# One decoder layer step: the sample tile's output products ahead of attention, from unsplit w_out rows, and the first full tile's products in attention's last turns

## The reference

```
proj = rmsnorm(x) @ w_in                      # q, k, v (8 heads x 64), b, c, u (512 channels each)
attn = dilated sliding-window attention       # windows (128,1) (512,4) (2048,16), merged by their sums
conv = b * conv3(c * u)
o    = concat(rmsnorm(attn, g_a), rmsnorm(conv, g_c)) @ w_out
x    = x + o
x    = x + moe(rmsnorm(x))                    # top-1 of 4 groups, top-2 of its 8 experts of width 512
y    = rmsnorm(x)
```

## Time and profile before

| | us |
|---|---|
| median of 3 runs | 1086.1 (1084.65 to 1086.41) |
| the profiled execution | 1085.33 |
| its span, first to last instruction | 1083.1 |
| PE busy in the span | 1051.1 (97%) |
| DVE busy | 448.0 (41%) |
| ACT busy | 272.8 (25%) |
| mean granted clock of PE | 0.994 of full speed |

### The profile page before, as it was taken

How to read it: one execution, slowest core, us unless ns; L and a number is a source line. 1 busy time by engine, 2 the same in 40 slices (tenths; PEclk the granted TensorE clock), 3 DMA queues, 4 the chain that set the end, 5 groups by cost and what they waited for, 6 DMA issues and landing times.

```text
span 1083.1 us, 19546 instructions
## 1 busy us (share of the span) xinstructions
PE 1051.1 (97%) x8052; PEld 684.3 (63%) x8052; DVE 448.0 (41%) x1100; ACT 272.8 (25%) x594; POOL 130.3 (12%) x167
## 2 busy tenths in 40 slices
PE   7999999999999999999999999999999999997987
PEld 6899999999967767888744433444434444443323
DVE  5414546233167657888864421212211111111156
ACT  7212221110137863323121111111111111111114
POOL 1001211002100000000112111121111112021010
PEclk9999999999999999999999999999999999999999
DMA  8216776234144206113999999999999999999987
GB/s 256 79 39 159 167 189 162 70 119 137 60 137 156 83 28 275 40 78 126 397 369 410 407 419 420 420 418 422 419 418 420 418 419 418 419 418 419 422 341 310
DMA packets 111133, 294.73 MB, mean 272 GB/s; under 512 B 43874, under 2 KB 68602, under 8 KB 86146
## 3 DMA queue, kind: packets, MB, share of 16 engines
q1 hardware_dynamic: 61634, 245.00, 56.9%
q0 software_dynamic: 14960, 40.03, 10.7%
q10 hardware_dynamic: 34448, 8.42, 3.5%
HBM read 276.38 MB, written 32.07 MB: 285 GB/s over the span
## 4 chain that ended last, share of the span: by engine, by line
PE 81%; DMA 7%; SPq 7%; DVE 3%; issue 1%; ACT 1%; DVEq 0%; POOLq 0%; ACTq 0%
PE psum L1292 15%; PE psum L916 9%; PE psum L918 8%; PE psum L917 8%; PE psum L1350 7%; SPq L782 6%; PE psum L1306 5%; PE psum L1050 3%; DMA expert_w<-in_w_up 3%; PE psum L1052 3%; PE psum L1051 3%; PE psum L1333 2%; PE psum L1276 2%; DMA y_tile<-y_rows 2%; PE psum L1001 1%
## 5 line engine op out<-in xcount | busy, mean ns | idle before, releaser
L1292 PE MATMUL psum<-expert_w,xT 128*64 128x512 f32 x512 | 228.9, 600 | 8.3 <-DMA expert_w<-in_w_up 8.1
L1294 PE MATMUL psum<-expert_w,xT 128*64 128x512 f32 x512 | 229.0, 600 | 0.0
L916 PE MATMUL psum<-h_hi,w_hi 128*128 128x344 f32 (+2 forms) x576 | 185.8, 323 | 3.0 <-DVE h_lo L1826 3.0
L918 PE MATMUL psum<-h_hi,w_lo 128*128 128x344 f32 (+2 forms) x576 | 184.0, 319 | 0.0
L917 PE MATMUL psum<-h_lo,w_hi 128*128 128x344 f32 (+2 forms) x576 | 183.9, 319 | 0.0
L1292 PEld LDWEIGHTS psum<-expert_w,xT 128*64 128x64 f32 x512 | 69.1, 138 | 145.6 <-issue 143.1
L1350 PE MATMUL psum<-expert_w,hT 128*64 128x512 f32 x512 | 116.9, 598 | 0.9 <-DVE hT L2425 0.9
L916 PEld LDWEIGHTS psum<-h_hi,w_hi 128*128 128x128 f32 x576 | 108.2, 188 | 5.4 <-DVE h_lo L1826 3.9
L917 PEld LDWEIGHTS psum<-h_lo,w_hi 128*128 128x128 f32 x576 | 108.3, 188 | 0.0
L918 PEld LDWEIGHTS psum<-h_hi,w_lo 128*128 128x128 f32 x576 | 108.2, 188 | 0.0
L2413 DVE TENSOR_TENSOR hid<-psum,silu_gate 64x512 f32<-64x512 f32 x32 | 21.8, 683 | 197.5 <-ACT silu_gate L1665 187.1
(11 more groups left out here) (335 smaller groups left out, 1383.2 us busy)
## 6 DMA issues: line engine op xcount, KB each, us to landing
expert_w<-in_w_gate SPq DMA_DIRECT2D x64, 1024.0 KB, 24.9
expert_w<-in_w_up SPq DMA_DIRECT2D x64, 1024.0 KB, 28.2
expert_w<-in_w_down SPq DMA_DIRECT2D x64, 1024.0 KB, 28.2
w_raw<-in_w_in SPq DMA_DIRECT2D x24, 512.0 KB, 5.3
y_tile<-y_rows SPq DMA_DIRECT2D x16, 512.0 KB, 13.0
kv<-in_cache_k POOLq DMA_DIRECT2D x24, 256.0 KB, 5.1
kv<-in_cache_v POOLq DMA_DIRECT2D x24, 256.0 KB, 4.7
x_tile<-in_x_prompt SPq DMA_DIRECT2D x8, 512.0 KB, 5.4
```

Source lines behind the costliest of these rows:

```text
L916: mm(ps, wh[:, k, :], h_hi[:, k, cols], start=(k == 0), stop=False)
L918: ins = mm(ps, wl[:, k, :], h_hi[:, k, cols], start=False, stop=(k == KD - 1))
L1292: mm(bank(0)[0:HEAD, :], xT[:, k, 0:HEAD], up[:, k, :], start=(k == 0), stop=(k == KD - 1), skip_group_check=True)
L1294: ins = mm(bank(0)[HEAD:P, :], xT[:, k, 0:HEAD], gate[:, k, :], start=(k == 0), stop=(k == KD - 1), skip_group_check=True)
```

## The change

The sample tile's output products no longer use the split w_out. Before the split one, w_out is loaded a second time, unsplit and without the gain (`load_wo_rows`, buffers wo_row0 to wo_row3, two row blocks for each step), and DVE multiplies the sample tile's 8 columns of qT and cT by the gain instead (`gain_sample`). So `project_sample(j)` has four products in place of eight. Steps 0 and 1 stand in the last projection tile, ahead of its last group; steps 2 and 3 in turn 1 of attention, ahead of its scores. They use bank 7, which attention needs later: ACT copies the sums away in its turn 2 (`hold_sample`, to the place of old query rows) and back to bank 5 in turn 18 (`bring_sample`).

In the place of the sample tile's products, three of the four sums of p=1 stand in turns 16, 17 and 18, whose order is now written out in `group_order[1]`; the fourth stands behind attention. The sample tile's sums of squares and their root move into attention (PE's turn 14, ACT's turn 15, `ROOT_AT`), and its transposes and routing products stand behind p=1's last sum and within p=2's first. SP loads the split rows only when the sample tile's steps have freed their buffers, and loads the residual input of p=1 and p=2 ahead of attention's end.

```diff
+        ROOT_AT = NSTEP - 2
+        group_order = [[(0, 1), (1, 1), (0, 0), (1, 0)], [(0, 1), (0, 0), (1, 1), (1, 0)]]
+        group_order += [[(0, 0), (0, 1), (1, 0), (1, 1)]] * (NT - 2)
...
+            load_wo_rows(0)
+            load_wo_rows(1)
+            sp.wait_ge(sample_projected, 1)
+            load_wo_rows(2)
+            sp.wait_ge(sample_projected, 2)
+            load_wo_rows(3)
...
             for k in range(KD):
+                if k == 0:
+                    sp.wait_ge(sample_projected, 3)
+                if k == 2:
+                    sp.wait_ge(o_ready, 4)
...
+            for t in turn[1:3] + turn[0:1] + turn[3:NT]:
+                if t == turn[0]:
+                    sp.wait_ge(masked, 4 * NSTEP)
+                if t == turn[3]:
+                    sp.wait_ge(pv_done, NSTEP)
...
+            def project_sample(j):
+
+                pe.wait_ge(s_attn, 4 if j == MA - 1 else 3)
+                for c in range(2):
+                    pe.wait_ge(wo_in[(2 * j + c) % 4], 16 * (j // 2) + 16)
+                for g, (half, c) in enumerate(group_order[0]):
+                    ins = mm(sample_out(g), s_gained[:, c * MA + j, :],
+                             wo_row[(2 * j + c) % 4][:, half * 512:(half + 1) * 512], start=(j == 0), stop=(j == MA - 1),
+                             skip_group_check=True)
...
+                if n == ROOT_AT:
+                    pe.wait_ge(masked, 4 * FREE_BANKS_FROM)
+                    square_sums(0)
+                if n == NSTEP:
                     pe.wait_ge(wo_ready, KD)
-                    pe.wait_ge(masked, 4 * FREE_BANKS_FROM)
-                if n >= PROJECT_AT:
-                    project_sample(n - PROJECT_AT)
+                    pe.wait_ge(a_ready, 1)
+                if n >= NSTEP:
+                    for k in range(MA):
+                        project(1, *group_order[1][n - NSTEP], k)
...
-            square_sums(0)
-            for p in range(1, NT):
+            square_sums(1)
+            for n in range(MA):
+                project(1, *group_order[1][3], n)
+            for pair in range(4):
+                turn_pair(0, pair)
+            for p in range(2, NT):
                 pe.wait_ge(a_ready, p)
                 for n in range(MA):
                     project(p, 0, 0, n)
+                    if p == 2 and n % 2 == 1:
+                        route_pair(0, n - 1)
+                        route_pair(0, n)
...
+            def hold_sample():
+
+                act.wait_ge(o_ready, 4)
+                act.wait_ge(q_out, 16)
+                act.wait_ge(scored, NS + 1)
+                nc.scalar.copy(s_held, bank(SAMPLE_BANK)).then_inc(sample_held, 1)
...
+            def gain_sample(k, x, lo, hi):
+
+                vec.tensor_tensor(s_gained[:, k + lo:k + hi, :], x[:, lo:hi, SEQ:NTOK],
+                                  gout[:, k + lo:k + hi].unsqueeze(2).broadcast_to([P, hi - lo, NS]), ALU.mult
+                                  ).then_inc(s_attn, 1)
```

More of the change, by code:

```diff
@@ L209, in program @@
         ssm = pack("ssm", [NS * H])[0:NS]
+        s_gained = pack("sample_gained", [KD, NS])
+        wo_row = [at("wo_row0", MISC + 12416, [D])] + [at(f"wo_row{i}", MISC + 16544 + 4096 * (i % 3), [D])
+                                                       for i in (1, 2, 3)]
+        s_held = at("sample_held", SROW, [512])
         pack = Pack(WEI, WEI + 16384)
@@ L1044, in project @@
                     pe.wait_ge(o_used, used_by(p - 1, half, c))
-                elif n == 0 and 2 * half + c == SAMPLE_BANK:
-                    pe.wait_ge(o_used, 4)
+                elif n == 0 and c == 0:
+                    pe.wait_ge(masked, 4 * NSTEP)
+                elif n == 0 and half == 1:
+                    pe.wait_ge(std_ac_ready, 1)
                 out = bank(2 * half + c)[0:w, :]
@@ L1095, in weigh_values, with square_sums @@
                 ins.then_inc(pv_done, 1)
+            def square_sums(p):
+                w = rows(turn[p])
+                pe.wait_ge(sq_summed, p + 1)
+                if p:
+                    pe.wait_ge(std_ac_ready, p)
+                for c in range(2):
+                    ins = mm(sums_out(p, w)[:, c:c + 1], sqs[p % 2][:, c, 0:w], ones[:, 0:1],
+                             start=True, stop=True)
+                ins.then_inc(ssq_ready, 1)
             for g in range(len(groups) - 4, len(groups)):
@@ L1113, in _ @@
                     weigh_values(n - 3)
-            def square_sums(p):
-                w = rows(turn[p])
-                pe.wait_ge(sq_summed, p + 1)
-                if p:
-                    pe.wait_ge(std_ac_ready, p)
-                for c in range(2):
-                    ins = mm(bank(6)[0:w, 2 * p + c:2 * p + c + 1], sqs[p % 2][:, c, 0:w], ones[:, 0:1],
-                             start=True, stop=True)
-                ins.then_inc(ssq_ready, 1)
             def turn_pair(p, pair):
@@ L1611, in _ @@
                     squares(1, (n - FIRST_AT,))
-            def roots(p):
-                w = rows(turn[p])
-                act.wait_ge(ssq_ready, p + 1)
-                if p >= 1:
-                    act.wait_ge(o_used, 4 * p)
-                nc.scalar.activation(std_ac[0:w, :], bank(6)[0:w, 2 * p:2 * p + 2], ACT.Sqrt, bias=eps[0:w, :],
-                                     scale=1.0 / DA).then_inc(std_ac_ready, 1)
+                if n == ROOT_AT + 1:
+                    roots(0)
             def root_ffn(p):
@@ L2128, in _ @@
                 recip_branch(p)
-                if p == 0:
-                    for half, c in first_groups:
-                        residual(0, half, (c,))
+                if p <= 1:
+                    for half, c in group_order[p]:
+                        residual(p, half, (c,))
                 else:
```

94 lines of the change are left out of this document (65 added, 29 removed).

## The result

The changed kernel took **1095.97 us** (median of four executions, 1094.58 to 1097.93), the kernel before 1086.26 (median of four, 1084.65 to 1086.66): a ratio of 1.0088, 95% interval 1.0072 to 1.0104, so 7.8 to 11.3 us slower. The forecast had been 1091.2 with a range up to 1094.5. The direction was right, the loss was larger than forecast, and the measured median lies 1.5 us above the range. The profiled execution of the changed kernel took 1094.58 us with a span of 1092.4; its partner of before took 1085.33 with a span of 1083.1.

A forecast was written before the change was run, and what follows sets the result against it. PE was taken to bound attention, and a VectorE and ScalarE chain behind its last weighing the third tile's start. Terms 5.2 - 3.35 + 0.9 + 2.0 + 0.7 = +5.4 us gave 1091.2 us, range 1086.5 to 1094.5.

The forecast's parts named there:

- Part 3: From attention's last weighing to the third tile: a 14.2 us chain replaces 17.55 us of PE work and waits, -3.35 us.
- Before, PE had 17.55 us: PE's work and waits in the kernel before, from 406.34 to the third tile's start at 423.89.
- moved as a whole: The 460 us expert stretch behind the output stage, DMA full, shifts by whatever happens ahead of it.
- Part 1: Ahead of attention and in turn 1: four sample steps of four products, 0.92 us each, delay attention's end by 3.7 us.
- W: End of the products of attention's last weighing of values, 406.34 us in the trace of before.
- Part 2: Attention's end: -7.4 sample products, +8.2 for p=1's groups, +0.24 sums, +0.45 gaps, so +1.5; W 5.2 us later.
- the slow clock: PE at the lower clock after its 1.94 us wait, counted inside the 17.55 us of before.
- Part 4: Inside the third tile (p=2): +0.9 us for sample routing, +2.0 for low clock after the wait, +0.7 for late DVE.
- Rival 2: Exponents, not PE, pace attention's first turns, so the 3.7 us ahead would hide: +1.7 us, 1087.7; chance 0.17.
- rival 3: PE's own queue decides the output stage: -7.3 us, 1078.5; chance 0.14 with cases between it and no change.
- rival 4: Split w_out rows reach ACT late in attention's turns 2 to 5: up to 3 us, 1094; chance 0.12.
- Rival 5: Each ACT table switch costs 2.7 us, not 1.3, in the chain and ahead of the last exponents: 1094.5; chance 0.07.

The follow-up runs named there:

- fillers at the end: Changed kernel with ten filler products in place of six behind the last expert's, ahead of the final mixing: 1093.77 us, ratio 1.0058.
- products doubled: Changed kernel with each of the sample tile's sixteen output products done twice, which changes that tile's result: 1096.56 us, ratio 1.0083.
- second timing: Changed kernel once more, unaltered, against the kernel before on the same chip: 1094.15 us (six executions) against 1087.99, ratio 1.0062.
- root late: Changed kernel with the sample tile's root moved behind the last turn's copies, one table load where there were three: 1091.88 us, ratio 1.0046.
- fillers ahead of p=2: Changed kernel with eight filler products in PE's wait ahead of the third tile's products: 1091.14 us, ratio 1.0034.
- early residuals: Changed kernel with the sample tile's four residuals moved ahead of attention's last division: 1089.95 us, ratio 1.0017.
- no fill: Changed kernel with all four of p=1's groups behind attention, none in turns 16 to 18: 1089.83 us, ratio 1.0019.
- no fill, early residuals: Changed kernel with p=1's groups all behind attention and the sample tile's residuals ahead of the last division: 1087.44 us against 1087.99, ratio 0.9991.
- the four edits: Changed kernel with p=1's groups behind attention, residuals before the last division, root behind the last copies, ten end fillers: 1083.45 us against 1086.74, ratio 0.9963.

## Why the prediction was off, step by step

The direction was right, and so was the mechanism in the output stage; the size was too small. The step that failed is how the kernel before was priced. Part 3's "Before, PE had 17.55 us" was read from one execution, with a stretch of low clock in it that two of four executions don't have, so that the term is -2.6 and not -3.35. And "it is moved as a whole by what happens ahead of it" left the final mixing, where the profiles of the changed kernel lose 1.3 us against those of before, without a term.

- **Part 1, +3.7: right within 0.4.** Steps of 0.92 us, and W + 3.5 for doubling them. Turn 2's transposes come 4.1 us later in the first pair of profiles.
- **Part 2, W at +5.2: right** (+5.3), though the 0.45 in it was too much: moving the root gave nothing back, and from turn 2's transposes to W it is 90.31 us against 89.07, +1.2 in place of +1.5. What I didn't see is that the last turns wait for ACT and DVE when the fill is gone, so that taking out the fill alone gives 4.4 us and not 8.2.
- **Part 3, the chain of 14.2 us: right**, with 14.24 us in both profiles of the changed kernel and with doubled products, 14.28 with fillers, 14.35 without fill, and with each part that I took out: residuals first 9.5 (411.79 to 421.30), one load fewer 12.96. **Its other side was wrong:** "Before, PE had 17.55 us" holds for some executions only. It includes "the slow clock", 1.4 us that two of four don't have. Between the four, W to p=2's start is 17.55, 16.12, 16.15 and 17.61 us (the sums of p=2 less 2.72), 16.86 on average, and the term is 14.24 - 16.86 = -2.6 and not -3.35.
- **Part 4, +0.9, +2.0, +0.7: right within 0.3 each on average**: 1.1 for the routing and 0.9 for DVE. For the clock, four executions with the same wait of 8.69 us lost 1.4, 2.7, 1.6 (with fillers at the end) and 1.8 us (products doubled), by the time from p=2's start to its sums less the 3.86 us at full clock: 1.9 on average.
- **"Moved as a whole":** the expert stage followed (from the fourth tile's sums to the fillers behind the last expert it is 605.0, 605.3 and 606.4 us in the three profiles of before, 605.4 and 605.9 in the two after). The mixing was in no term of the sum. It took 9.73 and 8.80 us for its first sixteen products after, and 7.10, 8.80 and 8.80 before: 1.0 us on average, 2.6 in the pair of profiles that were compared first. The wait ahead of it adds 0.3 on average and 0.8 in that pair.

With these sizes the sum is 5.3 - 2.6 + 1.1 + 1.9 + 0.9 = +6.6 us at the output stage, and +7.9 with the mixing. The terms come from the traces that they are compared with, so this is a check of the accounts and not a second forecast: the mean mark of the changed kernel (447.63, 448.89, and 447.72 with fillers at the end) is 6.7 us behind the 441.4 of before. That the first pair of profiles stood 5.5 us apart, next to the forecast 5.4, was partly luck: its reference had the low clock of 1.4 us, and its changed kernel one of the short ones. The two timings gave +9.7 (7.8 to 11.3) and +6.7 (1.0062 of 1087.5; 5.1 to 8.4). So of the 4.3 us between the sum's +5.4 and the first result, 1.2 are the output stage and 1.3 the mixing. The remaining 1.8 us no term explains, and the second timing lies 1.2 us below the corrected sum. I take both for the scatter of a few executions, which is argued and not shown. What speaks for it: two of the first four executions of the changed kernel had a mean clock of 0.987 and took 1097.4 and 1097.9 us, while the two others and the six of the second timing had 0.988 to 0.990 and took 1093.1 to 1095.1; and the four of before in the first timing, 1084.65 to 1086.66, all lie below the mean of the 62 later ones, 1087.7. The second timing's median, 1094.15, is even inside the forecast range. Whether the changed kernel has the low clock at the end more often than before isn't settled, but six of eight profiles against two of three give no sign of it.

The fourth tile's sums and the ratio tell how well the output stage carries through (mark less 442.10; and ratio less 1, times 1087.5; each mark is that of one execution, and 442.10 lies 0.7 us behind the mean of before):

| kernel | mark | time |
|---|---|---|
| changed, first measurement | +5.5 | +9.6 |
| changed, second measurement | +6.8 | +6.7 |
| fillers at the end | +5.6 | +6.3 |
| root late | +4.6 | +5.0 |
| fillers ahead of p=2 | +4.0 | +3.7 |
| early residuals | +2.1 | +1.8 |
| no fill | +1.2 | +2.1 |
| no fill, early residuals | -1.9 | -1.0 |
| the four edits | -4.1 | -4.0 |
| products doubled | +9.2 | +9.0 |

Of the nine below the first line none is off by more than 1 us: what the output stage gains or loses carries through. Rival 2 (start of attention not PE's) fell with W and with the doubled products, rival 3 (PE's queue decides) with the early residuals, rival 4 (split rows late) with the missing wait at 326.01. Rival 5 (2.7 us for a switch of tables) fell with the 1.28 us that one load fewer gave; the second 1.3 us of that price is seen in none of the runs.

## What to carry to other kernels

Moving work into the gaps of one stage only helps if the next stage doesn't wait for a chain that starts at that stage's end; count the chain first (here 14.2 us of VectorE and ScalarE), and leave as much of the bottleneck's work behind it as the chain is long. The same four steps in another place were worth more than the whole change: 3.1 us of residuals put into a wait of VectorE gave 4.6 us at the next tile. And before a term of 1 to 2 us is read from one profile, ask whether it is TensorE's clock: here its size, and behind waits of 2 to 4 us even whether it comes at all, changed between executions of one program, so such a term needs several profiles of it.

## What I had not expected of the hardware

- The same wait in the same program is followed by the low clock in some executions and not in others: 1.94 us ahead of p=1's second group, clock 0.50 behind it in two of four profiles and 1.00 in two. At the mixing, a wait of 2.75 us was followed by it and one of 3.00 us wasn't; among the variants waits of 2.69 and 2.78 us weren't, and those of 2.81, 3.00 and 3.03 were.
- Its length varies too: behind an equal wait of 8.69 us the clock was 0.50 until about 429.2 in one execution and until 432.0 in another; the lost time was 1.4 to 2.7 us in four.
- This makes up a part of the scatter. Of 62 timed executions of the kernel before, on three chips, 10 had a mean clock of 0.996 and took 1086.0 us on average, 8 had 0.995 and took 1087.0, 6 had 0.994 and took 1087.3, 25 had 0.993 and took 1087.8, 11 had 0.992 and took 1088.8, and 2 had 0.990 and took 1091.4. The groups overlap: the ten at 0.996 go from 1083.7 to 1089.1, so there are other causes, which no run here looked for.
